# Block of second projection and pooling: where GpSimd zeroes padded rows and splits the pooling's own weights

## The reference

```python
z = rmsnorm(x, g_mix[1]) @ w_in_pool          # 1024 -> 768 pooling channels + 256 query channels
ext = concatenate([prev15, u])                 # u = z[..., :768]
cs = cumsum(pad(ext))                          # trailing windows 2, 4, 8, 16 by channel group
pooled = (cs[t] - cs[t - w]) / count - u
mixed = einsum('blgc,gcd->blgd', pooled, w_pool_grp) * pool_scale
```

## Time and profile before

| | |
|---|---|
| median of 3 runs | 3249.93 us (3248.84 to 3257.4) |
| the profiled execution: its own time | 3255.0 us |
| its span | 3253.1 us |
| PE, PEld busy | 93%, 85% of the span |
| DVE, POOL, ACT busy | 48%, 29%, 25% |
| DMA | 68 GB/s on average |

### The profile page before, as it was taken

One profiled execution on the slowest core, in us unless ns is written; L12 is line 12 of the kernel. 1 busy time (PEld: TensorE's weight loads), 2 busy tenths in 40 slices (PEclk: granted clock), 3 DMA queues, 4 the chain that ended last, 5 costly groups with the idle time before them and its releaser, 6 DMA issues. The chain is left out here.

```text
span 3253.1 us, 51238 instructions
## 1 busy us (share of the span) xinstructions
PE 3024.3 (93%) x19509; PEld 2777.4 (85%) x19509; DVE 1555.6 (48%) x3312; ACT 817.7 (25%) x1508; POOL 952.2 (29%) x414
## 2 busy tenths in 40 slices
PE   5999967888888998999999999989899999999998
PEld 5999954555556668999999999989799999999998
DVE  4310215666655442575363453558418635626353
ACT  4101004666663331332020110122404301202010
POOL 2340000000000004444444444353134444444443
PEclk7997987999998998999999999999999999999999
DMA  4115622000005642111111111131311111111112
GB/s 156 46 32 188 216 88 107 1 2 1 1 23 187 194 123 107 50 40 42 49 44 40 46 38 53 35 118 37 121 39 57 39 46 46 39 52 36 48 40 84
DMA packets 126987, 220.39 MB, mean 68 GB/s; under 512 B 15946, under 2 KB 90556, under 8 KB 125648
## 3 DMA queue, kind: packets, MB, share of 16 engines
q1 hardware_dynamic: 108400, 201.55, 19.3%
q10 hardware_dynamic: 18432, 16.79, 1.6%
HBM read 202.58 MB, written 19.84 MB: 68 GB/s over the span
## 5 line engine op out<-in xcount | busy, mean ns | idle before, releaser
L394 POOL TENSOR_SCALAR weights_high<-weights_whole 128x1024 fp32r<-128x1024 f32 (+2 forms) x176 | 459.6, 2612 | 1150.8 <-PE banks L429 926.2
L425 PE MATMUL banks<-ffn_in_high,weights_high 128*128 128x364 f32 x2112 | 467.9, 330 | 16.7 <-DVE ffn_in_low L300 9.0
L427 PE MATMUL banks<-ffn_in_low,weights_high 128*128 128x364 f32 x2112 | 468.8, 330 | 0.0
L429 PE MATMUL banks<-ffn_in_high,weights_low 128*128 128x364 f32 x2112 | 468.4, 330 | 0.0
L396 POOL TENSOR_TENSOR weights_low<-weights_whole,weights_high 128x1024 fp32r<-128x1024 f32 (+2 forms) x176 | 385.6, 2191 | 26.1 <-issue 5.9
L425 PEld LDWEIGHTS banks<-ffn_in_high,weights_high 128*128 128x128 f32 x2112 | 368.5, 189 | 18.9 <-issue 18.8
L2598 DVE SCALAR_TENSOR_TENSOR conv_out<-conv_ext,conv_w,conv_out 128x1024 f32<-128x1024 f32 x176 | 320.6, 1822 | 113.3 <-ACT conv_out L2534 98.3
L429 PEld LDWEIGHTS banks<-ffn_in_high,weights_low 128*128 128x128 f32 x2112 | 369.3, 189 | 0.0
L427 PEld LDWEIGHTS banks<-ffn_in_low,weights_high 128*128 128x128 f32 x2112 | 368.5, 189 | 0.0
L2534 ACT ACTIVATE conv_out<-conv_ext,conv_b,conv_w 128x1024 f32<-128x1024 f32 (+1 forms) x176 | 138.3, 835 | 543.9 <-DVEq L2589 543.8
L2626 DVE TENSOR_TENSOR x<-x,banks 128x1092 f32 x64 | 82.7, 1292 | 393.5 <-PE banks L429 393.5
(11 more groups left out here) (388 smaller groups left out, 4687.8 us busy)
## 6 DMA issues: line engine op xcount, KB each, us to landing
weights_whole<-in_w_up SPq DMA_DIRECT2D x88, 512.0 KB, 3.5
past_rows<-in_kv_pages SPq DMA_DIRECT2D x160, 128.0 KB, 2.4
z<-in_kv_pages SPq DMA_DIRECT2D x96, 128.0 KB, 2.5
weights_whole<-in_w_down SPq DMA_DIRECT2D x32, 384.0 KB, 3.1
weights_whole<-in_w_down SPq DMA_DIRECT2D x32, 320.0 KB, 2.9
x<-in_cmp_pages ACTq DMA_DIRECT2D x64, 128.0 KB, 5.7
x<-in_cmp_pages SPq DMA_DIRECT2D x64, 128.0 KB, 5.5
cmp_rows<-in_cmp_pages ACTq DMA_DIRECT2D x64, 128.0 KB, 5.6
```

The lines of the kernel that those rows point to most:

```text
L394: pool.tensor_scalar(high, whole, 1.0, None, ALU.mult)
L425: pe.matmul(o, wh, high[:, at], start=kk == 0, stop=False)
L427: pe.matmul(o, wh, low[:, at], start=False, stop=False)
L429: last = pe.matmul(o, wl, high[:, at], start=False, stop=kk == len(terms) - 1)
```

## The change

GpSimd's list alone is reordered. The zeroing now stands behind the split of tile 2, not behind that of tile 1. (The comparison value is `w.parted`, which is 1 here: tile 0 came split from the stage before.) The split of the pooling's own weights now stands behind the split of tile 7, not behind that of tile 2. No instruction is added or removed, and no other engine's list is changed.

```diff
             for t in range(w.parted, NTILES):
                 w.part(k, pool, t, t // 2, t % 2, cols)
-                if t == w.parted:
+                if t == w.parted + 1:
                     pool.wait_ge(x_saved, 16 * KC)
                     tokens.wait_read(pool)
                     for n in range(2):
                         pool.memset(ext[n][:, 0:PST], 0.0)
                         pool.memset(held[n][:, TE:T], 0.0)
                     pool.drain().then_inc(zeroed, 1)
-                if t == w.parted + 1:
+                if t == NTILES - 1:
                     pool.wait_ge(loaded, 16 * (len(POOLING) + 3))
                     pool.tensor_scalar(wh[:], raw, 1.0, None, ALU.mult)
                     pool.drain()
                     pool.tensor_tensor(wl[:], raw, wh[:].bitcast(F32), ALU.subtract).then_inc(weights_split, 1)
```

## The result

| | before | changed |
|---|---|---|
| median, 14 runs each | 3252.86 us (3248.31 to 3257.4) | 3259.76 us (3251.04 to 3265.5) |
| profiled execution, its span | 3255.0, 3253.1 us | 3265.4, 3263.6 us |

The ratio is 1.0023, 95% interval 1.0013 to 1.0032, that is 4.2 to 10.4 us slower. Forecast were 3252.6 us and +2.7 us; the time lies above the stated range and the loss is over twice the forecast. It is still under the 0.3% named as the bound of "same". The kernel before has a median of 3252.86 us here, where three runs had given 3249.93; so 2.9 us of the distance to the range lie in the starting point, and the 6.9 us of loss are what has to be explained.

The account below looks back on a forecast made before the run. VectorE, held by GpSimd's splits, was taken to be the pacer once TensorE's hole closed. `group(0)` 0.7 us late plus 2.0 for the clock gave +2.7: 3249.93 + 2.7 = 3252.6 us, range 3246.0 to 3257.5.

Parts of the forecast that it names:

- What bounds it: In the stage, VectorE and not TensorE is the pacer once TensorE's 4.8 us hole before tile 3 is closed.
- Rival 2: All of TensorE's gain arrives, VectorE not being the pacer: -7.3 us, 3242.6 us; chance 0.03.
- (a): Tile 2's split ahead of the zeroing: squares' additions end 2.9 us later, the norm and VectorE's chain come 0.6 late.
- (b): Tile 3 split without the pooling's weights ahead: TensorE saves 7.3 us, VectorE's chain only 4.9; tile 4 waits 1.6.
- (c): Pooling's weights behind tile 7: TENSOR_SCALAR holds VectorE 1.8 us, TENSOR_TENSOR 4.7, counted as 6.2; `group(0)` 0.7 late.
- rival 3: Each hold on VectorE lasts as long as GpSimd's instruction: +7.4 us, 3257.3 us; chance 0.10.
- (d): A 4.9 us hole before `group(0)` lowers TensorE's clock, costing 2.0 us, between 0 and 2.57.
- my own extreme: The upper extreme of the prediction's summed terms, +8.5 us.

Follow-up runs that it names:

- the memsets: The changed kernel with the pooling's weights set to zero by two memsets instead of being split; ratio to the kernel before 0.9981.
- the second profile: The changed kernel, unaltered, profiled once more; one run, 3259.07 us.
- three pieces: The changed kernel with the pooling's weights split in three pairs of 768 columns at the same late place; ratios to the kernel before 0.9983 and 0.9985.
- early tile 2 alone: The kernel before with only the zeroing moved behind tile 2's split, the pooling's weights left in place; ratio to before 0.9991 (0.9979 to 1.0003).

## Why the prediction was wrong, point by point

**What bounds it: right.** VectorE was the pacer up to tile 7 once the hole before tile 3 was closed. Rival 2, TensorE's full 7.3 us, didn't arrive even with the memsets: groups started 5.2 us earlier.

**(a) Early split of tile 2: right.** The squares' additions took 10.93 us against 8.23, +2.7 for 2.9 forecast; the reciprocal started 31.74 us after the stage's first row against 31.21, +0.5 for 0.6. Tile 3's split waited for its DMA and started at 2178.2 on the scale of before, for 2176 to 2178. Nothing waited for that.

**(b) Tile 3 without the pair ahead: right.** The wait of the earlier trace rows is gone; take(2) came 4.4 us earlier, for 4.3; the hole before tile 4 was 1.5 us, for 1.6. The next two takes came 4.9 us earlier, 0.6 more than forecast.

**(c) The late pair: the step that failed, in one term.** The TENSOR_TENSOR was sized right: it held 4.77 us against 4.7. The TENSOR_SCALAR was scaled from the 0.8 us that 1024 columns hold to 1.8 us for 2304; it held 5.25. The scaling took for granted that the hold grows evenly with the columns, and at 1152 columns it is already 2.55. Together the pair held 10.0 and not 6.2 us. The text had 6.05, the whole duration, as upper bound, and rival 3 (+7.4 us, chance 0.10) is what happened in this term. I weighed it down by the addition at 2222.79 that ran free; that is true of 1024 columns and says nothing of 2304. The Trainium skill's page SBUF — State Buffer (Who interferes with whom) has the exclusion last for the whole instruction. At 768 and 1024 columns the rows of the TENSOR_SCALAR disagree (0.48 of 2.13 us held, 0.69 of 2.77); at 1152 and 2304 it nearly holds (2.55 of 3.13, 5.25 of 6.04).

The place was off too. I had the TENSOR_SCALAR's hold before take(5) and the TENSOR_TENSOR's behind it. Both fell before it: with 5.25 us more, VectorE hadn't yet reached take(5) when the TENSOR_TENSOR began. Take(5) came 5.1 us later than before where 2.5 earlier was forecast, and the hole opened before tile 7 (8.5 us) and not before the groups (4.9). The groups then waited for tile 7 itself, which ended at 114.1 on TensorE, while take(6) had ended at 112.3.

**(d) The clock: right in kind.** Tile 7 took 13.4 and 14.8 us, 1.4 and 2.8 over 12.0; forecast was 2.0, with 2.57 as the upper end, which the second profile passes. The group start was thus 4.8 to 6.3 us late, against 2.7 forecast for the two together.

**From stage to median.** Behind the groups' start the stretch to its end took 33.4 us in the profile before and 31.8 in both after; over all the kernels it took about 30.3, 31.8 or 33.4, whatever the edit, by how long the clock was low in it (in three pieces twice: 30.4 and 33.5). That gave back 1.6, so the stage was 3.3 and 4.7 us longer in the two profiles. The medians say 4.2 to 10.4. The group start, 4.8 to 6.3, lies in that interval. It is the fairer number if the stretch behind is long or short by chance in either kernel; the two profiles of three pieces point that way, but the kernel before has one profile only, so this isn't shown. Whether something else adds to the median's 6.9 stays open: outside the stage the instructions are the same, and in the twelve profiles the time ahead of it varies by 16 us and the time behind it by 2.7 (960.6 to 963.3).

**The range.** 3246.0 to 3257.5 failed for the same term, and because I let a chance of 0.10 for the rival stand where only a row of other size spoke against it. Two more faults added to it. Its upper end lies below my own extreme, 3249.93 + 8.5 = 3258.4. And it stood on a median of three runs that fourteen put 2.9 us higher: 3249.93 + 6.9 = 3256.8 would lie inside.

## What to carry to other kernels

When GpSimd's work is moved off TensorE's path, look at what VectorE does beside its new place: here the pair of 11 to 12 us held no VectorE instruction beside copies out of PSUM and a one-input reciprocal (early tile 2 alone) and held 10 us beside window sums. Cut GpSimd's TENSOR_SCALARs over on-chip memory to 1024 columns or fewer where VectorE is busy with two such inputs; with pieces of 768 the change went from slower than before to faster (1.0023 to 0.9983 and 0.9985), partly because one piece happened to meet a take from PSUM. And don't scale a price from a row of one size to another size when the upper bound gives another sign or over twice the result: give the bound its chance.

## What the runs showed of the hardware that was not expected

A float32 TENSOR_SCALAR of GpSimd held a VectorE instruction with two on-chip inputs, issued 0.2 us behind it, by 0.48 us at 768 columns (duration 2.13), 0.69 at 1024 (2.77), 2.55 at 1152 (3.13) and 5.25 at 2304 (6.04). The time from letting VectorE in to the instruction's end follows the columns beyond full 1024s: 0.38 us for 128, 0.60 for 256, 0.81 for 384, 1.45 for 768, 1.88 for 1024. An instruction issued behind this point ran undisturbed (with 1.6 us or less left of 1024 columns, 1.2 of 768). Its two-input TENSOR_TENSOR held to within 0.2 us of its end at every size that was met, 256 to 2304 columns. Memsets of 2304 columns held nothing.
